# A triangular inverse whose products run as diagonal blocks: four 32x32 matmuls, or two 64x64, in place of one 128x128

## What is computed

```python
lmat = jnp.where(strict, jnp.einsum('bhncd,bhnsd->bhncs', kb, kc) * decay, 0.0)
rhs = jnp.concatenate([vc * bc[..., None], kb * jnp.exp(gc)[..., None]], axis=-1)
sol = lax.linalg.triangular_solve(lmat + jnp.eye(CHUNK, dtype=f32), rhs, left_side=True, lower=True)
```

## Time and profile before

| what | value |
|---|---|
| runs | 3293.69, 3294.92, 3295.84 us, median 3294.92 |
| the profiled execution, its own time | 3295.94 us |
| its span, first to last instruction | 3294.2 us |
| mean granted TensorE clock | 0.858 |
| busy: PE, DVE, POOL, ACT | 2803.7, 1341.8, 1031.4, 898.7 us |
| chain that ended last: PE, DVE, ACT, issue | 57%, 15%, 5%, 5% of the span |
| the heads | from 430.8 us (first L633) to 1388.8 us (L1085) |

### The profile page before, as it was taken

The page is one execution under the profiler, slowest core; times in us unless marked ns, Lnnn a source line. Parts: engine busy times, 40 slices in busy tenths (PEclk is TensorE's granted clock), DMA queues, the critical chain, the costliest instruction groups (busy, mean ns, idle before and its releaser), DMA issues.

```text
span 3294.2 us, 44660 instructions
## 1 busy us (share of the span) xinstructions
PE 2803.7 (85%) x17169; PEld 2519.2 (76%) x17169; DVE 1341.8 (41%) x1868; ACT 898.7 (27%) x1333; POOL 1031.4 (31%) x357
## 2 busy tenths in 40 slices
PE   7599978888888888679999997966699999999993
PEld 3399967777777777579999996965688877787882
DVE  0400055475465466423111213344255554445554
ACT  0200123232222322202101102002255455454543
POOL 1255220221121022234646643631123222223222
PEclk9799876785786686689999998987599999999997
DMA  8333631011011011011212211211366566665665
GB/s 294 99 112 124 277 130 57 18 57 41 19 54 41 25 48 54 27 51 51 80 55 76 91 56 46 69 51 38 109 201 194 184 211 200 201 202 186 198 190 176
DMA packets 446079, 362.05 MB, mean 110 GB/s; under 512 B 13953, under 2 KB 398986, under 8 KB 446026
## 3 DMA queue, kind: packets, MB, share of 16 engines
q1 hardware_dynamic: 427946, 320.70, 30.9%
q10 hardware_dynamic: 15200, 30.15, 2.5%
q0 software_dynamic: 2880, 10.49, 0.8%
HBM read 310.69 MB, written 50.60 MB: 110 GB/s over the span
## 4 chain that ended last, share of the span: by engine, by line
PE 57%; DVE 15%; ACT 5%; issue 5%; DMA 1%; ACTq 0%; POOL 0%; DVEq 0%; POOLq 0%; SPq 0%
PE psum L585 22%; PE psum L803 8%; PE psum L569 8%; PE psum L785 3%; DVE m_prod L1633 3%; DVE m_lo L424 2%; PE psum L722 2%; PE psum L739 2%; PE psum L714 2%; PE psum L729 2%; PE psum L633 1%; PE psum L787 1%; PE psum L745 1%; DVE cy L1307 1%; DVE gu L1628 1%
## 5 line engine op out<-in xcount | busy, mean ns | idle before, releaser
L785 PE MATMUL psum<-he,m_hi 128*128 128x384 f32 x1584 | 485.4, 377 | 67.4 <-DVE m_lo L424 66.2
L424 POOL TENSOR_TENSOR m_lo<-m_raw,m_hi 128x2048 fp32r<-128x2048 f32 (+1 forms) x55 | 251.5, 4572 | 724.7 <-ACT m_hi L1122 724.7
L465 POOL TENSOR_TENSOR w_hi<-raw,zero 128x2048 fp32r<-128x2048 f32 (+2 forms) x68 | 249.2, 3664 | 683.5 <-PE psum L585 583.8
L585 PE MATMUL psum<-a_hi,w_hi 128*128 128x320 f32 x1728 | 401.1, 314 | 63.6 <-DVE a_lo L1209 32.6
L787 PE MATMUL psum<-he,m_lo 128*128 128x192 f32 x1584 | 409.0, 258 | 0.0
L585 PE MATMUL psum<-a_lo,w_hi 128*128 128x320 f32 x1728 | 397.6, 312 | 0.0
L585 PE MATMUL psum<-a_hi,w_lo 128*128 128x320 f32 x1728 | 397.3, 311 | 0.0
L501 POOL TENSOR_TENSOR ml<-lt,level 128x640 f32<-128x640 f32 x80 | 125.1, 1570 | 793.8 <-PE psum L569 793.4
L785 PEld LDWEIGHTS psum<-he,m_hi 128*128 128x128 f32 x1584 | 313.8, 198 | 76.5 <-issue 74.3
L585 PEld LDWEIGHTS psum<-a_hi,w_hi 128*128 128x128 f32 x1728 | 291.9, 190 | 72.5 <-issue 41.1
L468 POOL TENSOR_TENSOR w_lo<-raw,w_hi 128x2048 fp32r<-128x2048 f32 (+2 forms) x68 | 329.0, 4839 | 5.3
(11 more groups left out here) (287 smaller groups left out, 4562.5 us busy)
## 6 DMA issues: line engine op xcount, KB each, us to landing
m_raw<-in_moe_w_dram SPq DMA_DIRECT2D x276, 512.0 KB, 4.5
raw<-in_mod_w_dram SPq DMA_DIRECT2D x48, 512.0 KB, 3.9
raw<-in_ffn_w_dram SPq DMA_DIRECT2D x44, 512.0 KB, 4.6
mod_raw<-in_mod_w_dram SPq DMA_DIRECT2D x16, 1024.0 KB, 5.3
raw<-in_dn_w_in_dram SPq DMA_DIRECT2D x32, 512.0 KB, 4.3
m_raw<-in_moe_w_dram SPq DMA_DIRECT2D x54, 256.0 KB, 2.8
raw<-in_sc_w_in_dram SPq DMA_DIRECT2D x24, 512.0 KB, 4.2
rows_in<-raw SPq DMA_DIRECT2D x23, 512.0 KB, 7.3
```

What stands on the lines that cost most here:

```text
L424: eng.tensor_tensor(m_lo[q][:, 0:n], m_raw[q][:, 0:n], m_hi[q][:, 0:n].bitcast(F32), ALU.subtract)\
L465: pool.tensor_tensor(w_hi[s][:, 0:cols], raw[s][:, 0:cols], zero[:, :].broadcast_to([P, cols]), ALU.add)\
L585: mm = pe.matmul(psum[:, 4 * s + 2 * m + a, 0:HALF], w[:, k, m, :], v[:, k, a * HALF:(a + 1) * HALF], start=(k == 0 and n == 0), stop=(k = ...
L785: pe.matmul(psum[:, bank, 0:2 * CAP], wh[:, c:c + P], he[:, k, :, :].rearrange("p v c -> p (v c)"), start=(k == 0), stop=False)
```

## The change

Products of levels 1 to 5 are computed on diagonal blocks only. `blocks(l)` gives the four slices of 32 for levels 1 to 4, since a block of the inverse is at most 32 wide after level 4, and the two slices of 64 for level 5. TensorE issues one matmul per block and tile: rows R of the operands, columns R of the result, which lands in the partitions R. The copies on ScalarE and the updates on VectorE become one instruction per block, over all 5 tiles. What lies outside the blocks is no longer written. Semaphores count as before: only the last instruction of a group increments. Head 1 to 7 become straight code on TensorE; on the other engines they stay a loop.

```diff
+        def blocks(l):
+            n = 32 if l < 5 else CH
+            return [slice(i, i + n) for i in range(0, P, n)]
...
+            def block_mm(l, k, lhs, rhs, name):
+
+                for t in range(TT):
+                    for R in blocks(l):
+                        mm = pe.matmul(wide(k)[R, t * P + R.start:t * P + R.stop], lhs(t)[R, R], rhs(t)[R, R],
+                                       start=True, stop=True)
+                mm.then_inc(sem(name), 1)
...
-                            tile_mm(2 * d, lambda t: ml[:, d, t, :], lambda t: xx[:, d, t, :], "p")
+                            block_mm(l, 2 * d, lambda t: ml[:, d, t, :], lambda t: xx[:, d, t, :], "p")
...
-                            tile_mm(2 * d + 1, lambda t: xt[:, d, t, :], lambda t: pp[:, d, t, :], "xm")
-                        tile_mm(2 * d, lambda t: pp[:, d, t, :], lambda t: xt[:, d, t, :], "xtm")
+                            block_mm(l, 2 * d + 1, lambda t: xt[:, d, t, :], lambda t: pp[:, d, t, :], "xm")
+                        block_mm(l, 2 * d, lambda t: pp[:, d, t, :], lambda t: xt[:, d, t, :], "xtm")
...
-            with pe.Fori(1, H) as h:
+            for h in range(1, H):
                 head(h, True)
...
-                        act.activation(pp[:, d, :, :], tiles(wide(2 * d)), ACT.Copy).then_inc(sem("pcopy"), 1)
+                        for R in blocks(l):
+                            cp = act.activation(pp[R, d, :, R], tiles(wide(2 * d))[R, :, R], ACT.Copy)
+                        cp.then_inc(sem("pcopy"), 1)
...
-                            dve.tensor_tensor(xx[:, d, :, :], xx[:, d, :, :], tiles(wide(2 * d + 1)), ALU.subtract)\
-                                .then_inc(sem("xup"), 1)
+                            for R in blocks(l):
+                                up = dve.tensor_tensor(xx[R, d, :, R], xx[R, d, :, R], tiles(wide(2 * d + 1))[R, :, R],
+                                                       ALU.subtract)
+                            up.then_inc(sem("xup"), 1)
...
-                        dve.tensor_tensor(xt[:, d, :, :], xt[:, d, :, :], tiles(wide(2 * d)), ALU.subtract)\
-                            .then_inc(sem("xtup"), 1)
+                        for R in blocks(l):
+                            up = dve.tensor_tensor(xt[R, d, :, R], xt[R, d, :, R], tiles(wide(2 * d))[R, :, R],
+                                                   ALU.subtract)
+                        up.then_inc(sem("xtup"), 1)
```

## The result

The changed kernel takes **3347.33 us** (median of four runs, 3343.26 to 3356.86) against 3294.31 us for the kernel before (four runs), a ratio of **1.0166** (95% interval 1.0143 to 1.0188). The forecast was 3340, in a range of 3296 to 3400. The profiled execution took 3346.75 us, its span is 3345.0 us and its mean granted clock 0.805, where it was 0.858. One execution of a later run, e10, took 6874.44 us at a granted clock of 0.36 and is left out of that run's numbers.

The account below looks back on a forecast made before the run. TensorE was taken to set the inversion's pace, VectorE adding two of four updates. Eight heads of 3.9 (stage) plus 2.1 (scan), less 1.8 and 1.4, gave +44.8 us: 3340 us, range 3296 to 3400.

Parts of the forecast that it names:

- One product: TensorE, inversion stage: four blocks of a tile abreast at half clock take 0.58 us a product; ends 0.29 and 2.34.
- The rival by which they don't: TensorE products: blocks not abreast, or not all four, so TensorE keeps the pace; 3365 to about 3590 us; chance 0.20.
- An update: VectorE, inversion stage: each block update moves to other partitions, 0.355 us apart; a level's sixteen fill 5.65 us.
- The rival in which they overlap at 0.24: VectorE updates: starts 0.24 us apart, sixteen fill 3.95 us; about 3285 us, 3240 with full clock; chance 0.11.
- Levels 3 and 4: Inversion stage: three products, then sixteen updates on the chain; 7.98 us a level, +0.3 each.
- Level 2: Inversion stage: reciprocal of the last head's output no longer covered, VectorE sets the pace; 9.74 for 7.71 us, +2.0.
- The clock: TensorE, inversion stage: products on part of the array run at half clock, and the scan starts at it.
- the clock stays full: Inversion stage and scan: products 0.29 to 0.45 us, scan loses nothing; 3296 to 3303 us; chance 0.14.
- The scan: Scan after the inversion: first three steps of 4.53 us at half clock in place of 11.50 together; +2.1 us a head.
- I count nothing, as they come ahead of need: TensorE's instruction fetch for straight-code heads: set at zero, though a hundred more packets, each a stall, would be 150 us.
- PE idle for instructions within a product: Inversion-stage products in the profile after: listed as one of the signs that the forecast is wrong; no size.
- The register steps: TensorE, before a head's first product: straight code gives back 0.2 us for each of seven heads, -1.4 us.

Follow-up runs that it names:

- e10: 20 real matmuls of 128x2 (80 instructions) put ahead of head 0 on TensorE, on the kernel of e2; 3340.37 us, ratio 1.0146.
- e3: The kernel before with only ScalarE's copies and VectorE's updates cut into blocks, products whole, heads in the loop; 3371.77 us, ratio 1.0230.
- e4: The kernel of e2 with copies and updates whole again, so blocks on TensorE alone; 3274.32 us, ratio 0.9929.
- e5: The kernel of e2 with VectorE's updates reordered block by block, xx then xt on the same 32 partitions; 3322.60 us, ratio 1.0070.
- e8: 64x64 blocks at all levels, results kept packed so copies and updates are not cut, heads in the loop; 3181.16 us, ratio 0.9652 to the kernel before.
- e2: The changed kernel with TensorE's heads 1 to 7 in the loop again and an empty instruction taking the waits before each product group; 3326.88 us, ratio 1.0092.
- e1: The kernel before with only TensorE's heads 1 to 7 unrolled into straight code; 3293.62 us, ratio 0.9992.
- e11: The kernel of e2 with the 32x32 blocks' results kept packed in the same columns, so most copies and updates are whole; 3303.67 us, ratio 1.0022.
- e9: 62 real matmuls of 128x2 (248 instructions) put ahead of head 0 on TensorE, on the kernel of e2; 3365.90 us, ratio 1.0214.
- e6: 96 empty instructions put ahead of head 0 on TensorE, on the kernel of e2; 3325.73 us, ratio 1.0095.
- e7: 176 empty instructions put ahead of head 0 on TensorE, on the kernel of e2; 3326.63 us, ratio 1.0099.

## Why the prediction was right, and where it was not

**The outcome** (3347 against 3340) and the main mechanism hold: VectorE's sixteen cut updates take the chain over from PE. e3 and e4 show it from both sides: the cuts alone (ScalarE's copies with them) cost 75 us, and without them the block products win 22.

**One product**, 0.58 us: 0.52 measured. The blocks run abreast at the half clock. The rival by which they don't is out. The rule of the Trainium skill that it went by ("TensorEngine Tiling (Array Packing)", "Restrictions and Gotchas"), that different row tiles cannot access the same PSUM bank at once, does not hold for these blocks, which write different partitions of one bank: a product takes 0.52 us, not 2.34. The Trainium skill's floor of about 25 ns between starts ("TensorE: Matmul & The Clock Gate", "Back-to-back issue gap") is not seen either: 40 rows in 0.52 us are 13 ns apart.

**An update**, 0.355 us from start to start: 0.333 measured, 5.33 us for a level's sixteen. The rival in which they overlap at 0.24 needs the same partitions, as e5 shows. Levels 3 and 4, said to be 7.98, are 7.6 to 7.7 where no gap is on the chain.

**Level 2**, 9.74 with the reciprocal on the chain: 9.55. **Level 1**, 9.66: 8.45 to 9.0. Here the clock is still 1.00 (to 969 in the fifth head), which the sum had not given it. **Level 5**, 5.2: 4.7 to 4.8.

**The clock** fell as assumed: 0.50 to 0.54 from 969 to 1000 in the fifth head. The rival "the clock stays full" is out. But the reason given, matmuls on part of the array, was too wide: e8's 64x64 products run at 0.93 to 1.00. Whether it is the narrow blocks or PE's idle time between them is not shown, as no run has 32x32 blocks without it (PE is busy for 46 to 63% of such stages). **The scan** was said to start at half clock and lose 2.1 us a head. It lost 1.6 by these traces. In six heads the first step takes 4.5 us, as said; in the fifth and the sixth the clock comes up again in level 5 (0.78 in the fifth's first step), and that step takes 3.5 to 3.6 us. The third step takes 4.35 us at half clock, not 4.53, and four of the eight heads before had longer scans than the one that was read (43.9 against 43.2 us). The size is loose: against e1, whose scan is that of the kernel before, the loss would be 2.7.

**What failed** is the sentence "I count nothing, as they come ahead of need", on the fetch. It was read from products of 1.17 us, for which it is true (e1: nothing lost with 67 packets). Block products of 80 instructions in 0.52 us use up 254 rows in 1.7 us, and no two packets come less than 2.97 us apart in any run. The gaps are up to 2.1 us each; with the packets' ends at other places, the fifth head takes 42.6 us where the third takes 38.1, and e2 is 20 us faster as a whole. The forecast had named this as a sign of being wrong, PE idle for instructions within a product, and it is the one of its signs that came. **The register steps**, -1.4 us, are not to be seen: e1 cannot be told from no change, and the first stages are 3.6 us longer, for which no run shows the cause.

So the mechanism is right, and that the total came within 8 us is partly luck, because errors cancel: the levels were set some 2.4 us a head too long (by the third head) and the scan 0.5, and the fetch, within the heads and behind them, was set at nothing.

## What to carry to other kernels

Diagonal blocks on TensorE cut every copy and update behind them into as many pieces, unless the blocks of a tile are stored in the same columns; so count the instructions of the engines that read the result before those of TensorE. The smaller block need not be the faster: 64x64 packed gave 0.58 us a product at full clock with 40 instructions, 32x32 gave 0.52 at half clock with 80, and even packed (e11) it left the kernel no faster than before. Where a trace shows "issue" within a row of equal instructions, compare its places with the fetch queue's packets, and expect time to change with edits that merely move code: some 35 us of e9's span, besides the added matmuls themselves.

## What the runs showed of the hardware that was not expected

- The loop of the kernel before, 1422 instructions of TensorE a head, is fetched once and kept (no packet from 652 to 1407 us); that of e2, 2953 instructions, is fetched again in every pass (130 packets), and so is that of e8, 2037 (108).
- An edit far ahead can open a gap far behind: 3.40 us at 1776.83 in the changed kernel, in a section that it doesn't touch. The part behind the heads took 1917.1 us before, 1925.7 after and 1931.3 in e9.
- 64x64 blocks, two abreast, keep the granted clock at 0.93 to 1.00 over a stage, in all eight heads of e8; 32x32 blocks, four abreast, with PE busy for about half of the time, leave it at 0.51 to 0.63.
- 96 and 176 empty instructions ahead of head 0 left every gap of head 0 at its row (e6, e7); 20 real matmuls moved them by the 80 instructions that they are (e10). Why the empty ones did not count is open.
